# Two transformer layers on one core: other order of first loads, one bank for c and b_s, earlier splits after the values, a later gated norm, and the selection's choices inside the attentions

## The chip, the cores and the metric

The kernel runs on one core of one Trainium2 chip. The metric is the device time of one execution, in microseconds, from a run without or with the profiler; the profiler's span, from the first to the last instruction, is some 2 us shorter. PE is TensorE (PEld its weight loads), DVE VectorE, ACT ScalarE, POOL GpSimd, SP SyncE, whose queue issues every DMA.

## The reference

A first layer on x (1024 positions of 1024) projects x by `w_in` into a gated MLP part, a differential attention of 4 heads and a selective attention of 4 heads. The last two matter here:

```python
u = gelu(u); v = layer_norm(gelu(v).reshape(..., 4, 64), ln_g, ln_b)   # gated part: v is normed in groups of 64
out_a = u * (einsum('gts,bnsgc->bntgc', masked_w_s, v) + b_s)          # by blocks of 128 positions
score = einsum('bth,bths->bts', wi * idx_scale, relu(qi . ki))         # index scores, 8 heads of 32
score = where(allowed, score, -inf)
_, sel = lax.top_k(score, 256)                                         # ties: the first positions win
attention of 4 heads over the 256 selected keys of each query
```

Then come the output projection, layer norm, a gated FFN of 2816 and layer norm; a second layer, whose vectors depend on silu(c) @ w_cond, has a stick-breaking attention, a pooling mixer and another such FFN. All products are made of fp32 operands split in a high and a low part, three products each.

## The kernel before

Each engine's program is written out by hand as a list of calls (`pe_program`, `act_program`, `dve_program`, `pool_program`, `sp_program`, from L2734); semaphores join them. So the order on each engine is fixed, and an instruction that waits holds all behind it. All edits lie in the first fifth of the time.

**First loads** (`sp_first`, L647): x comes in eight blocks of 128 rows, x0 to x7. PE turns each (L564), ACT copies the high part (L575), DVE subtracts the low part (L582). Weights come as units of 128 x 1024: SP loads one into one of three `raw` buffers (L434), ACT copies its high part into one of five `wh` (L485), POOL subtracts for `wl` (L502). `sp_feed`, `act_feed` and `pool_feed` do this as far ahead as the buffers allow; a load waits for the split of the unit three before it, a split for the last use of the unit five before it. The third unit (the index keys) is loaded by four small DMAs. After x5, x6 and x7 the products of the three index units for positions 0 to 511 follow, then c and the gated part's w_s and b_s are turned (L676 to L685) and the other halves of the index products made. ACT applies Silu to c (L696), out of c's bank.

**Projections** (steps s = 0 to 47, `projects`): 0 to 7 give u and v of the gated part ("a"), 8 to 15 the values ("b"), 16 to 39 queries and keys, two halves to each unit, 40 to 47 the values of the selective attention ("c"). The list `turns` (L890) says in which order the five streams are called: 0 the selection, 1 the projections, 2 the gated norm (eight turns: four "var", four "norm", `NORM_STEPS`), 3 the four gated products, 4 first halves of the first ten projections. ACT copies each result out of its bank; for s from 16 to 39 DVE makes the low part `prl` (L997) and frees the bank. PE has four banks for projections. At the last step of a kind (m == 7) ACT begins with `act_feed(..., leave=1)`, which splits the units that follow.

**Selection** (stream 0): 20 score tiles, two at a step (PE L1038, ACT L1055 relu, DVE L1067 and L1070), then 31 steps of a binary search for the 256th score, a bit each: DVE counts four of the six blocks of queries (blocks 2 to 5; L1097), ACT two (6 and 7; L1089). Step 38 ends it. Then `dve_choose` (L1187) makes, for each block, five instructions over 128 (i + 1) columns: equal (L1192), running count (L1195), ties beyond need (L1198), below (L1202), bias (L1206). Blocks 2 to 5 follow at steps 40, 42, 44, 46, with `running` as the place of their counts, blocks 6 and 7 in the attentions, with `tcum`.

**Attentions** (`pe_attend`, `act_attend`, `dve_attend`, L1455 to L1507): 48 events, one to a place t; 0 to 7 are head 0 of the differential attention, 8 to 23 head 1 and pair 0 of the selective one in turn. At place t PE makes the logits of t (L1294), weighs the values for t - 4 (L1384) and turns the probabilities of t - 2 (L1358). DVE reads the logits of t out of their banks (L1319), ends the sums of t - 1 (L1336 to L1344), then, at places 1 to 10, makes one instruction of a choice. Block i's choice is read by event ("c", 0, i), from place 13 on.

Of the kernel before, what the change touches and what calls it, by code (L numbers as in the profile page):

```python
# [15 lines left out]
ACT = mybir.ActivationFunctionType  # L16
# [12 lines left out]
NRAW = 3  # L29
# [143 lines left out]
def build(nc, T, out):  # L173
    with ExitStack() as top:
# [93 lines left out]
        sg, powers = sb("sg", 128), sb("powers", 32)  # L268
        running = res[:, 7168:8192]

# [376 lines left out]
        def sp_first():  # L647
            sp.i.dma_start(con[:, :], T["consts"]).then_inc(*con_in.up("con", 16))
            for tb in range(8):
                if tb >= 6:  # L650
                    sp.wait_ge(*mm.after(("x", tb - 6, 1)))
                sp.i.dma_start(x_bufs[tb % 6], xd[128 * tb:128 * tb + 128, :]).then_inc(*x_in[tb % 6].up(("x", tb), 16))
                if tb == 3:
                    sp_feed(-1, NRAW)
            sp.i.dma_start(nd[:, :], T["dist"]).then_inc(*nd_in.up("nd", 16))
# [10 lines left out]
        def pe_first():  # L666
# [8 lines left out]
            pe.wait_ge(*small_in.after("c"))  # L675
            pe.i.transpose(bank[:, 0:8], score[0:8, 0:128], idn[0:8, 0:8]).then_inc(*mm.up("c"))  # L676
            bank = X["r"].open("ws")
            pe.wait_ge(*X["r"].prior("ws"))
            pe.wait_ge(*gmlp_in.after("bs"))
            for g in range(4):  # L680
                last = pe.i.transpose(bank[:, 128 * g:128 * g + 128], tmp[:, 128 * g:128 * g + 128], idn)
            last.then_inc(*mm.up("ws"))
            bank = X["r"].open("bs")
            pe.wait_ge(*X["r"].prior("bs"))
            pe.i.transpose(bank[:, 0:4], b4, idn[0:4, 0:4]).then_inc(*mm.up("bs"))  # L685

        def act_first():
            for tb in range(8):
                act_turn("x", tb, xh)
                if 3 <= tb < 6:  # L690
                    act_feed(-1, most=tb - 2)
                if tb >= 5:
                    act_index(0, tb - 5)
            act_feed(-1)
            act.wait_ge(*mm.after("c"))
            act.i.activation(cc[:, :], uses.held["c"][:, 0:8], ACT.Silu).then_inc(*av.frees(uses, "c"))  # L696

# [3 lines left out]
        def dve_first():  # L701
            for tb in range(8):
                dve_turn("x", tb, xh, xl)
                if tb >= 5:
                    dve_index(0, tb - 5)
            dve.wait_ge(*mm.after("ws"))
            dve.i.tensor_copy(wst, uses.held["ws"][:, :]).then_inc(*dv.frees(uses, "ws"))
            wv = wst[64:128, :].rearrange("p (g s) -> p g s", g=4)[:, :, 0:64]
            dve.wait_ge(*dv.now())
            dve.i.memset(wv, 0.0).then_inc(*dv.up("wst"))  # L710
            dve.wait_ge(*mm.after("bs"))
            dve.i.tensor_copy(bsc[:, 0:4], uses.held["bs"][:, 0:4]).then_inc(*dv.frees(uses, "bs"))

# [177 lines left out]
        for s in range(N_PROJECT):  # L891
# [4 lines left out]
            else:  # L896
                turns += [0, 1] if s < 39 or s % 2 == 0 else [1]
            if 2 <= s < 10:
                turns.append(2)
            if FIRST_BITS + 1 <= s < FIRST_BITS + 5:  # L900
                turns.append(3)
# [57 lines left out]
        def act_project():  # L959
            for s, (n, m, half) in enumerate(projects):  # L960
# [20 lines left out]
                if half is not None or m < 7 or s == N_PROJECT - 1:  # L981
                    act_feed(project_released(s))
                yield

# [17 lines left out]
        def sp_project():  # L1002
            for s, (n, m, half) in enumerate(projects):
# [11 lines left out]
                elif n != "a":  # L1015
# [3 lines left out]
                                   ).then_inc(*stage_out[s % 4].up(("v", s), 16))  # L1019
                if s == QK0 + 1:  # L1020
                    sp_gmlp()
# [130 lines left out]
        def dve_topk():  # L1152
# [29 lines left out]
            yield  # L1182
            for n in range(4):
                rest(dve_choose(n, running))
                yield
# [300 lines left out]
        def dve_attend():  # L1486

            last_choices = chain(dve_choose(4, tcum), dve_choose(5, tcum), repeat(None))
            for t in range(N_PLACES):
# [8 lines left out]
                if u is not None:  # L1498
                    dve_sums(u)
                    next(last_choices)  # L1500
                h = last_block(t, 5)
# [1407 lines left out]
```

## Time and profile before

| what | us |
|---|---|
| median of three runs (lowest, highest) | 2557.81 (2553.99, 2559.68) |
| the profiled execution, its own time | 2555.43 |
| its span | 2553.6 |
| PE busy in the span | 2416.5 (95%) |
| DVE busy | 1502.8 (59%) |
| ACT busy | 933.2 (37%) |
| POOL busy | 691.0 (27%) |
| mean granted clock of PE | 0.973 |

Busy times are those of the whole span; the stretches below each have a limit of their own. Granted clock 1.00 is 2.4 GHz, 0.50 is 1.2 GHz. An idle time in brackets with an arrow names what ended it.

### The profile page before, as it was taken

Reading aid. Unit: us, or ns where it says so; the run is one execution under the profiler, and the core shown is the slowest. Engines: PE = TensorE matmul, PEld = TensorE weight load, DVE = VectorE, ACT = ScalarE, POOL = GpSimd, SP = SyncE. Lnnn points to the kernel's source line nnn. Section 1 sums busy time; section 2 is a strip of 40 time slices with the busy share of each in tenths; the row PEclk is TensorE's granted clock in tenths of the full one; section 3 lists DMA queues with packets and bytes.
Section 4 is the critical chain, followed back from the end, with each engine's and each line's share of the span. In section 5 each row is a group of like instructions: output and inputs, shape, how many; then the busy total and the mean of one; then the engine's idle time right before and its main releaser. Section 6 shows DMA issues by size and latency. Waiting matters only on the chain.

```text
span 2553.6 us, 31471 instructions
## 1 busy us (share of the span) xinstructions
PE 2416.5 (95%) x12119; PEld 1954.8 (77%) x12119; DVE 1502.8 (59%) x2557; ACT 933.2 (37%) x1704; POOL 691.0 (27%) x389
## 2 busy tenths in 40 slices
PE   7989988889999999999999989888989999999998
PEld 6667877778888777778887866666768888888886
DVE  2698988762766777763239037775466555544225
ACT  3556636661223232332113225554433333232112
POOL 2012210001135444542223211011224454442220
PEclk9999988989999999999999999998989999999999
DMA  5014542213314454454222210001322223233233
GB/s 163 17 50 139 200 149 88 96 58 136 117 58 132 149 173 154 152 181 173 90 104 80 79 42 18 26 17 67 99 91 69 88 73 93 83 132 116 99 107 116
DMA packets 216717, 260.01 MB, mean 102 GB/s; under 512 B 16348, under 2 KB 145900, under 8 KB 216568
## 3 DMA queue, kind: packets, MB, share of 16 engines
q1 hardware_dynamic: 216568, 258.00, 30.8%
q8 instruction: 96, 1.57, 0.3%
q14 instruction: 53, 0.43, 0.1%
HBM read 198.14 MB, written 59.82 MB: 101 GB/s over the span
## 4 chain that ended last, share of the span: by engine, by line
PE 72%; DVE 17%; ACT 3%; DMA 3%; issue 2%; POOL 1%; SPq 1%; POOLq 0%; DVEq 0%; ACTq 0%
PE bank L545 9%; PE bank L547 9%; PE bank L546 9%; PE bank L1876 7%; PE bank L1877 7%; PE bank L1878 7%; PE bank L521 5%; PE bank L523 5%; PE bank L522 5%; DVE rest L2492 2%; PE bank L1384 2%; DVE junk L1097 2%; DVE res L1319 2%; PE bank L564 1%; DVE took L2497 1%
## 5 line engine op out<-in xcount | busy, mean ns | idle before, releaser
L502 POOL TENSOR_TENSOR wl<-raw,wh 128x1024 fp32r<-128x1024 f32 x117 | 298.1, 2564 | 1354.2 <-ACT wh L485 1354.1
L545 PE MATMUL bank<-wh,yh 128*128 128x512 f32 x768 | 301.5, 393 | 4.3 <-POOL wl L502 1.7
L547 PE MATMUL bank<-wh,yl 128*128 128x512 f32 x768 | 299.2, 390 | 0.0
L546 PE MATMUL bank<-wl,yh 128*128 128x512 f32 x768 | 299.2, 390 | 0.0
L497 POOL TENSOR_TENSOR wl<-res,wh 128x512 fp32r<-128x512 f32 x144 | 198.4, 1400 | 146.8 <-ACT wh L482 123.4
L485 ACT ACTIVATE wh<-raw 128x1024 fp32r<-128x1024 f32 x117 | 122.8, 1056 | 304.8 <-PE bank L547 287.1
L1876 PE MATMUL bank<-yh,wh 128*128 128x512 f32 x576 | 225.2, 391 | 0.0
L1878 PE MATMUL bank<-yh,wl 128*128 128x512 f32 x576 | 224.2, 389 | 0.0
L1877 PE MATMUL bank<-yl,wh 128*128 128x512 f32 x576 | 224.1, 389 | 0.0
L497 POOL TENSOR_TENSOR wl<-raw,wh 128x512 fp32r<-128x512 f32 x108 | 157.2, 1469 | 231.6 <-ACT wh L482 231.6
L2009 DVE TENSOR_TENSOR res<-bank,res 128x512 f32<-128x512 f32 x144 | 99.6, 692 | 136.2 <-PE bank L1878 128.4
L2075 DVE TENSOR_TENSOR res<-bank,res 128x512 f32<-128x512 f32 x96 | 65.0, 689 | 184.8 <-PE bank L547 184.8
L545 PEld LDWEIGHTS bank<-wh,yh 128*128 128x128 f32 x768 | 144.5, 188 | 36.6 <-issue 5.3
L547 PEld LDWEIGHTS bank<-wh,yl 128*128 128x128 f32 x768 | 144.3, 188 | 30.1
L546 PEld LDWEIGHTS bank<-wl,yh 128*128 128x128 f32 x768 | 144.5, 188 | 29.4
L521 PE MATMUL bank<-yh,wh 128*128 128x512 f32 x384 | 153.9, 401 | 2.9 <-DVE ql L2388 1.4
L482 ACT ACTIVATE wh<-res 128x512 fp32r<-128x512 f32 x144 | 83.5, 623 | 192.7 <-DVE res L469 141.6
L522 PE MATMUL bank<-yl,wh 128*128 128x512 f32 x384 | 151.0, 393 | 0.0
L523 PE MATMUL bank<-yh,wl 128*128 128x512 f32 x384 | 151.0, 393 | 0.0
L1876 PEld LDWEIGHTS bank<-yh,wh 128*128 128x128 f32 x576 | 108.1, 188 | 29.9 <-issue 4.3
L1878 PEld LDWEIGHTS bank<-yh,wl 128*128 128x128 f32 x576 | 108.1, 188 | 22.7
L1877 PEld LDWEIGHTS bank<-yl,wh 128*128 128x128 f32 x576 | 108.1, 188 | 22.1
(339 smaller groups left out, 5418.6 us busy)
## 6 DMA issues: line engine op xcount, KB each, us to landing
early<-in_w_cond SPq DMA_DIRECT2D x96, 256.0 KB, 2.9
raw<-in_w_gu SPq DMA_DIRECT2D x44, 512.0 KB, 4.1
raw<-in_w_down SPq DMA_DIRECT2D x44, 512.0 KB, 3.6
raw<-in_w_in SPq DMA_DIRECT2D x40, 512.0 KB, 4.2
qk_d<-res SPq DMA_DIRECT2D x36, 512.0 KB, 4.3
raw<-in_w_gate SPq DMA_DIRECT2D x22, 512.0 KB, 4.1
raw<-in_w_up SPq DMA_DIRECT2D x22, 512.0 KB, 4.3
res<-in_x SPq DMA_DIRECT2D x16, 512.0 KB, 8.6
```

What stands on the lines that cost most here:

```text
L485: act.i.activation(wh[n % NU][:, :], raw_of(u)[:, :], ACT.Copy).then_inc(*av.up(("wh", u)))
L497: pool.i.tensor_tensor(wl[n % NU][:, half], src, wh[n % NU][:, half].bitcast(F32), ALU.subtract).then_inc(*po.up(("wl", u)))
L502: pool.i.tensor_tensor(wl[n % NU][:, :], raw_of(u)[:, :], wh[n % NU][:, :].bitcast(F32), ALU.subtract).then_inc(*po.up(("wl", u)))
L521: pe.i.matmul(bank[:, :], a, a_h[:, s], start=k == 0, stop=False)
L522: pe.i.matmul(bank[:, :], a, a_l[:, s], start=False, stop=False)
L523: last = pe.i.matmul(bank[:, :], b, a_h[:, s], start=False, stop=k == 7)
L545: pe.i.matmul(bank[:, 0:wide], xa, h[:, c:c + wide], start=k == 0, stop=False)
L546: pe.i.matmul(bank[:, 0:wide], xa, l[:, c:c + wide], start=False, stop=False)
L547: last = pe.i.matmul(bank[:, 0:wide], xb_, h[:, c:c + wide], start=False, stop=k == nk - 1)
L1876: pe.i.matmul(bank[:, :], h[:, c:c + 128], high[:, k, :], start=k == 0, stop=False)
L1877: pe.i.matmul(bank[:, :], h[:, c:c + 128], low[:, k, :], start=False, stop=False)
L1878: last = pe.i.matmul(bank[:, :], l[:, c:c + 128], high[:, k, :], start=False, stop=k == 3)
```

## The change

First loads: one unit before x4, the second after x5, the third after x7 (before: three before x4). c's bank: b_s is turned into the same bank as c; DVE copies both out, and ACT's Silu works in place. Values' successors: at step 14 ACT also makes the splits that step 15 began with, after its two bits. The gated norm's turns move from steps 2 to 9 to steps 7 to 14, the gated products from 11 to 14 to 26 to 29, the stores of out_a from step 17 to step 30. Choices: all thirty instructions lie in `dve_attend`, with `tcum`, after the sums at places 5 to 22: min(30, 30 (t - 4) // 18) of them are made by place t.

```diff
@@ -266,7 +266,6 @@
         junk = sb("junk", 1024, BF, 512)
         junk_a = sb("junk_a", 1024, BF, 512)
         sg, powers = sb("sg", 128), sb("powers", 32)
-        running = res[:, 7168:8192]
 
 
         area(low)
@@ -650,8 +649,9 @@
                 if tb >= 6:
                     sp.wait_ge(*mm.after(("x", tb - 6, 1)))
                 sp.i.dma_start(x_bufs[tb % 6], xd[128 * tb:128 * tb + 128, :]).then_inc(*x_in[tb % 6].up(("x", tb), 16))
-                if tb == 3:
-                    sp_feed(-1, NRAW)
+                if tb in (3, 5):
+                    sp_feed(-1, tb // 2)
+            sp_feed(-1, NRAW)
             sp.i.dma_start(nd[:, :], T["dist"]).then_inc(*nd_in.up("nd", 16))
             sp.i.dma_start(score[0:8, 0:128], T["c_2"].rearrange("(k p) -> k p", p=128)).then_inc(*small_in.up("c", 16))
             for n, nm in ((0, "gmlp_ln_g"), (1, "gmlp_ln_b")):
@@ -673,16 +673,14 @@
             bank = X["r"].open("c")
             pe.wait_ge(*X["r"].prior("c"))
             pe.wait_ge(*small_in.after("c"))
-            pe.i.transpose(bank[:, 0:8], score[0:8, 0:128], idn[0:8, 0:8]).then_inc(*mm.up("c"))
+            pe.i.transpose(bank[:, 0:8], score[0:8, 0:128], idn[0:8, 0:8])
+            pe.wait_ge(*gmlp_in.after("bs"))
+            pe.i.transpose(bank[:, 8:12], b4, idn[0:4, 0:4]).then_inc(*mm.up("c"))
             bank = X["r"].open("ws")
             pe.wait_ge(*X["r"].prior("ws"))
-            pe.wait_ge(*gmlp_in.after("bs"))
             for g in range(4):
                 last = pe.i.transpose(bank[:, 128 * g:128 * g + 128], tmp[:, 128 * g:128 * g + 128], idn)
             last.then_inc(*mm.up("ws"))
-            bank = X["r"].open("bs")
-            pe.wait_ge(*X["r"].prior("bs"))
-            pe.i.transpose(bank[:, 0:4], b4, idn[0:4, 0:4]).then_inc(*mm.up("bs"))
 
         def act_first():
             for tb in range(8):
@@ -692,8 +690,8 @@
                 if tb >= 5:
                     act_index(0, tb - 5)
             act_feed(-1)
-            act.wait_ge(*mm.after("c"))
-            act.i.activation(cc[:, :], uses.held["c"][:, 0:8], ACT.Silu).then_inc(*av.frees(uses, "c"))
+            act.wait_ge(*dv.after("c"))
+            act.i.activation(cc[:, :], cc[:, :], ACT.Silu).then_inc(*av.up("c"))
 
         def pool_first():
             pool_feed(-1)
@@ -703,13 +701,14 @@
                 dve_turn("x", tb, xh, xl)
                 if tb >= 5:
                     dve_index(0, tb - 5)
+            dve.wait_ge(*mm.after("c"))
+            dve.i.tensor_copy(bsc[:, 0:4], uses.held["c"][:, 8:12]).then_inc(*dv.up())
+            dve.i.tensor_copy(cc[:, :], uses.held["c"][:, 0:8]).then_inc(*dv.frees(uses, "c"))
             dve.wait_ge(*mm.after("ws"))
             dve.i.tensor_copy(wst, uses.held["ws"][:, :]).then_inc(*dv.frees(uses, "ws"))
             wv = wst[64:128, :].rearrange("p (g s) -> p g s", g=4)[:, :, 0:64]
             dve.wait_ge(*dv.now())
             dve.i.memset(wv, 0.0).then_inc(*dv.up("wst"))
-            dve.wait_ge(*mm.after("bs"))
-            dve.i.tensor_copy(bsc[:, 0:4], uses.held["bs"][:, 0:4]).then_inc(*dv.frees(uses, "bs"))
 
 
 
@@ -895,9 +894,9 @@
                 turns += [0, 0, 1] if s % 2 else [0, 1]
             else:
                 turns += [0, 1] if s < 39 or s % 2 == 0 else [1]
-            if 2 <= s < 10:
+            if 7 <= s < 15:
                 turns.append(2)
-            if FIRST_BITS + 1 <= s < FIRST_BITS + 5:
+            if 26 <= s < 30:
                 turns.append(3)
         vbufs = [res[:, 6144 + 512 * i:6656 + 512 * i] for i in range(4)]
         staged = [b[:, :].bitcast(F32) for b in (*prh, *prl)]
@@ -980,6 +979,10 @@
                                      ).then_inc(*av.up(("project", s)))
                 if half is not None or m < 7 or s == N_PROJECT - 1:
                     act_feed(project_released(s))
+
+
+                if (n, m) == ("b", 6):
+                    act_feed(project_released(s + 1), leave=1)
                 yield
 
         def pool_project():
@@ -1017,7 +1020,7 @@
                     wide, c = (512, 0) if n == "b" else (256, 512)
                     sp.i.dma_start(T["v_d"][128 * m:128 * m + 128, c:c + wide], staged[s % 4][:, 0:wide]
                                    ).then_inc(*stage_out[s % 4].up(("v", s), 16))
-                if s == QK0 + 1:
+                if s == QK0 + 14:
                     sp_gmlp()
                 if s == QK0 + 5:
                     sp_load_head(0)
@@ -1180,8 +1183,7 @@
             dve.wait_ge(*dv.now())
             dve.i.tensor_scalar(need, cnt, -1.0, 256.0, ALU.mult, ALU.add).then_inc(*dv.up())
             yield
-            for n in range(4):
-                rest(dve_choose(n, running))
+            while True:
                 yield
 
         def dve_choose(n, sums):
@@ -1485,7 +1487,11 @@
 
         def dve_attend():
 
-            last_choices = chain(dve_choose(4, tcum), dve_choose(5, tcum), repeat(None))
+            choices = chain.from_iterable(dve_choose(n, tcum) for n in range(6))
+
+            def chosen_by(t):
+                return min(30, max(0, 30 * (t - 4) // 18))
+
             for t in range(N_PLACES):
                 if t < N_EVENT:
                     dve_logits(t, 0)
@@ -1497,7 +1503,8 @@
                 u = lagging(t, 1)
                 if u is not None:
                     dve_sums(u)
-                    next(last_choices)
+                    for _ in range(chosen_by(t) - chosen_by(t - 1)):
+                        next(choices)
                 h = last_block(t, 5)
                 if h is not None:
                     dve_subln(h)
```

## Rows read from the trace of the kernel before

**Rows 1.** The page: the span, and the chain that ended last by engine
```profile
span 2553.6 us, 31471 instructions
...
PE 72%; DVE 17%; ACT 3%; DMA 3%; issue 2%; POOL 1%; SPq 1%; POOLq 0%; DVEq 0%; ACTq 0%
```

**Rows 2.** Windows: busy us (and instructions) of each engine in six stretches
```profile
core 0: us, PE busy (x) PEld busy (x) DVE busy (x) ACT busy (x) POOL busy (x), PEclk, DMA share, GB/s
80.00:142.00 62.00, 61.41 (x432) 44.22 (x430) 50.31 (x91) 40.45 (x87) 0.00 (x0) 1.00 0.01 1
142.00:164.00 22.00, 15.61 (x102) 10.89 (x102) 20.20 (x24) 14.31 (x23) 10.26 (x4) 0.92 0.34 88
...
221.00:341.00 120.00, 120.00 (x526) 99.19 (x525) 102.69 (x282) 75.64 (x123) 32.63 (x14) 0.99 0.59 198
...
366.70:408.20 41.50, 30.56 (x180) 24.04 (x181) 37.75 (x96) 24.08 (x66) 4.17 (x2) 0.71 0.45 155
408.20:460.50 52.30, 46.65 (x350) 38.45 (x349) 39.70 (x131) 37.40 (x88) 0.00 (x0) 0.90 0.21 69
460.50:472.80 12.30, 12.05 (x102) 10.76 (x103) 4.17 (x22) 8.43 (x25) 0.00 (x0) 1.00 0.05 10
```

**Rows 3.** Timeline of the first loads: start, us, engine, line, [idle before <-releaser]
```profile
3.08 11.44 SPq L434 DMA_DIRECT2D raw<-in_w_in  x6
...
19.62 1.97 PE L564 MATMUL bank<-con,res 128*128 128x128 f32 x8 [4.47 <-DMA res<-in_x]
22.25 1.94 PE L564 MATMUL bank<-con,res 128*128 128x128 f32 x8 [0.65 <-DVE xl L582]
```

**Rows 4.** Timeline around c's Silu
```profile
45.49 1.28 ACT L696 ACT_TABLE_LOAD   x1
47.02 0.26 PE L685 MATMUL bank<-con,res 4*128 4x4 f32 x1 [3.33 <-ACT cc L696]
48.23 0.63 PE L523 MATMUL bank<-xh,wl 128*128 128x512 f32 x1
```

**Rows 5.** Timeline: the last of lambda's loads, and the reduction on DVE
```profile
52.38 0.43 SPq L1239 DMA_DIRECT2D sg<-in_diff_subln_g  x1
57.34 2.40 DVE L1245 CUSTOM_DVE_ANT_0 score<-score 128x64 f32<-128x64 f32 x1
```

**Rows 6.** Timeline: a norm step on DVE beside three splits on POOL
```profile
143.28 7.73 POOL L502 TENSOR_TENSOR wl<-raw,wh 128x1024 fp32r<-128x1024 f32 x3 [72.80 <-ACT wh L485]
147.03 0.69 DVE L815 TENSOR_REDUCE res<-res 128x8 f32<-128x512 f32 x1 [0.42 <-ACT res L968]
148.73 2.82 DVE L819 TENSOR_TENSOR res<-res 128x512 f32<-128x512 f32 x1
```

**Rows 7.** Timeline: a gated product, the successors' splits, and two waits
```profile
183.89 1.02 PE L861 MATMUL bank<-res 128*128 128x512 f32 x2
216.55 2.93 ACT L485 ACTIVATE wh<-raw 128x1024 fp32r<-128x1024 f32 x3
220.24 0.76 PE L521 MATMUL bank<-xh,wh 128*128 128x512 f32 x1 [6.26 <-POOL wl L502]
232.56 0.69 DVE L997 SCALAR_TENSOR_TENSOR prl<-bank,prh 128x512 fp32r<-128x512 f32 x1 [4.51 <-DMA v_d<-prl]
```

**Rows 8.** Timeline: first and last of 20 and of 10 choices; first logits
```profile
348.50 0.42 DVE L1192 TENSOR_SCALAR junk<-score,cand 128x384 bf16<-128x384 f32 x1
365.38 0.96 DVE L1206 SCALAR_TENSOR_TENSOR score<-score,nd 128x768 f32<-128x768 f32 x1
365.39 0.33 PE L1294 MATMUL bank<-kh,qh 64*128 64x128 f32 x2
366.26 0.28 DVE L1319 CUSTOM_DVE_ANT_0 res<-bank,nd 128x128 f32<-128x128 f32 x1
371.31 0.69 DVE L1192 TENSOR_SCALAR junk<-score,cand 128x896 bf16<-128x896 f32 x1
407.09 1.23 DVE L1206 SCALAR_TENSOR_TENSOR score<-score,nd 128x1024 f32<-128x1024 f32 x1
```

## The prediction

> **What bounds the kernel now.** I read the page first: a span of 2553.6 us whose last-ending chain is mostly TensorE (PE), with 17% of VectorE (DVE) [rows 1]. All edits lie before 475 us, so I cut that part into stretches and compared the busy time of the engines [rows 2]. From 80 to 142 us (score tiles and first projections) PE is busy 61.41 of 62 us: PE sets the pace, and what DVE does beside it is free. From 142 to 164 PE is busy 15.61 of 22 us and DVE 20.20: DVE sets it. From 221 to 341 PE is busy 120.00 of 120. In the attentions, 366.7 to 408.2 (places 1 to 10) has DVE at 37.75 of 41.5 us and PE at 30.56; 408.2 to 460.5 (places 11 to 23) has PE at 46.65 of 52.3 and DVE at 39.70. So each moved DVE instruction is worth what its old stretch gives back, less what its new one takes.
>
> **First loads: 3.8 us gained.** SP spends 3.08 to 14.52 us issuing three units of weights (six DMAs, four of them small pieces), and only then issues x4. PE idles 4.47 us and turns x4 at 19.62 [rows 3]. Now one unit is loaded ahead of x4 and x5. PE turned x3 at 13.2 and turns are 2.6 us apart (22.25 - 19.62, the row's start times), so x4 can be turned at 15.8: 3.8 us earlier. The third unit comes after x7, but its product starts only two products of 6.3 us after the first one, and its split takes 3.4 us.
>
> **c's bank: 5.7 us gained.** PE now waits 3.33 us before the turn of b_s (L685), since its bank holds c until ACT has loaded a table (1.28 us) and run Silu (L696) [rows 4]. After that the clock is at 1.2 GHz: twelve matmuls come every 0.427 us instead of 0.2275 (one of them is the 48.23 row), 2.4 us. With c and b_s in one bank, freed by a DVE copy, both go. What is late next is DVE: its lambda reduction waits for a load issued at 52.38 and then takes 2.40 us beside a split on POOL [rows 5], and it stands ahead of the copies that free PE's index banks. That load follows POOL's splits, which come 3.8 us earlier; the banks come free at about 56.1 and PE wants the first at 56.7. So the whole start gains 3.8 + 3.3 + 2.4 = 9.5 us, 6 if that chain is late.
>
> **The gated norm, later: a loss in DVE's chain.** Each of four variance steps holds four passes of 0.69 us and two small ones (3.2 us), each norm step three passes and a reciprocal (2.4 us); L815 is such a pass [rows 6]. Five steps, 14.4 us, run before 146.5 us under PE's cover. Moved behind step 7 of the projections they lose it: DVE would reach the end of that step's tiles near 143 (PE's own pace sets it, and the split on POOL that holds one pass) instead of 146.5, then owes 14.4 us more, in the stretch where DVE is the pace. The four gated products on DVE (3.0 us) leave this stretch. DVE's last bit of projection step 15 is then later by 14.4 - 3.5 - 3.0 = 7.9 us, at 226.2 instead of 218.3.
>
> **The successors' splits: the stall goes, another comes.** ACT splits three units at 216.55, after the two bits of step 15; PE stands idle 6.26 us until 220.24 [rows 7]. One step earlier this ends near 217.8 even with DVE's delay. But PE needs its banks back: the bank of projection 17 is freed by DVE after `prl` 17, which today waits 4.51 us for a store of v (DMA v_d<-prl, DVE at 232.56) [rows 7]. SP issues that store behind raw loads that wait for POOL's fourth split, and ACT makes this split after bit 16, about 12.6 us after the last bit of step 15. From 226.2 that is 238.8, and PE's projection 21 starts at 239.5 where it now starts at 237.8: a loss of 1.7 us in all, the saved stall included. Bounds: a gain of 7.5 (stall 6.3, cold matmuls 1.2) if DVE keeps up, a loss of 7 if it doesn't.
>
> **The gated products on PE: 3.5 us lost.** The four fp32 products (L861) make a projection last 6.34 us instead of 5.46, 0.88 each, now in a stretch where PE had slack (it stalled at 214 anyway) [rows 7]. At steps 26 to 29 PE has none [rows 2]: 4 x 0.88 = 3.5. The stores of out_a, now at step 30, are far ahead of their readers: nothing.
>
> **A collision: 2.3 us.** When three splits ran on POOL from 143.28 to 151.0, a DVE tensor_tensor (L819) took 2.82 us instead of 0.69 [rows 6]. The last norm step has three such passes and now starts near 215.6, where the three moved splits run; today these meet counts, which aren't held up. Each pass could lose about 1.8: 0 to 5.4 us, and I take 2.3, since the alignment is good to some us only. The Trainium skill (SBUF — State Buffer, Who interferes with whom) says that a DVE instruction with two SBUF inputs and a GpSimd instruction that reads SBUF lock each other out for a whole instruction. By that rule all three passes would wait, and the term would be 5.4; the L819 row agrees with it.
>
> The middle sums to 1.7 + 3.5 + 2.3 = 7.5 us lost, with bounds of 4 gained and 13 lost.
>
> **The choices.** Twenty instructions (blocks 2 to 5), 348.50 to 366.34, leave the end of the projections. There PE runs on until its first logits at 365.39, and DVE's first follows at 366.26 [rows 8]: they were covered, and at most 0.9 us comes back, counted at nothing. Ten more (blocks 6 and 7), 371.31 to 408.32, are in the attentions already [rows 8]; they last 13.0 us. Now all thirty, 17.1 + 13.0 = 30.0 us (by width a block costs 3.2, 3.9, 4.6, 5.4, 6.1, 6.8), are dealt over places 5 to 22, one, two, two, one and so on. Place by place, DVE's other work is what it was. Places 1 to 7 lose 9.1 us of choices and get 3.2: with PE's own limits (it runs at half clock there, mean 0.71 [rows 2]) 4.8 are gained. Places 8 to 10 are even. Places 11 to 23 get 23.0 and 0.7 of gaps, and of DVE's 12.6 us of idle there [rows 2] 9.4 are waits (the rest are gaps of 0.03 us between instructions): 14.3 lost. From place 24 to 27, DVE now waits for PE's backlog DVE busy 4.17 of 12.3 [rows 2]; PE will have less of it, which returns some 1.9. That leaves 14.3 - 4.8 - 1.9 = 7.6; PE's shadow of exp and turns at the wide places, and its clock, cost more. I add 2.4 for these, from one spell at 1.2 GHz as after b_s. The choices cost 10 us; bounds 4 (every idle used) and 18 (two or three more spells at half clock).
>
> **Sum.** -9.5 + 7.5 + 10.0 = +8.0 us. The profiled execution took 2555.43 us (1.8 around its span), so 2563.4; the median of the three runs is 2557.81, 2.4 above it, and on that base the forecast is 2565.8.
>
> **Rivals.**
> Chance 0.45: the forecast, DVE is the pace in both new places.
> Rival A, faster, 0.15: the idle time absorbs the choices. DVE has 3.75 us idle in 366.7 to 408.2 and 12.6 in 408.2 to 460.5 [rows 2], 16.4 together, nearly the 17.1 that come. If the attentions cost 2 and the middle 0, -9.5 + 2 = -7.5: 2550.3. Against it: the idle is in pieces between waits, the first part is not where choices land, and choices stand between sums and the next logits.
> Rival B, no change, 0.25: the attentions cost 10, but the middle is even, because the norm's 14.4 us fit into waits of DVE for PE or because the collision is missed: -9.5 + 0 + 10 = +0.5: 2558.3. It decides if `prl` 17 is not later against step 7 than now.
> Rival C, clearly slower, 0.15: PE, idle at places 12 and 13 where DVE gets 2.4 + 1.7 us of choices beside 3.9 + 5.5 of its own, falls to 1.2 GHz, then at places 19 to 23 too, where its work (4 to 6 us a place) doubles and PE becomes the pace. Three more spells at the 2.4 us of the one after b_s, and the full 5.4 of collision: 8.0 + 7.2 + 3.1 = +18.3, 2576.1. It decides when the granted clock of 408.2 to 460.5 falls below 0.85 (now 0.90).
>
> Faster by over 0.2% (5.1 us, about what a measurement here can tell from none): 0.15 (A). Within: 0.27 (B and a small part of the forecast). Slower: 0.58. The range holds the forecast, B and most of C: 2552.5 to 2576.
>
> **What would show it.** Right: x4's turn at 15.8, no gap before L685, the first scores 9.5 us earlier; the wait on `wl` at 220 gone but PE waiting for ACT's or DVE's bank frees around steps 17 to 21; L861 inside the full stretch; DVE at over 95% from place 8 to 23 and PE waiting for its logits and sums. Wrong: PE's first logits over 5 us earlier than 365.39 - 2.0, which would mean the norm cost nothing, or places 11 to 23 done in under 58 us (52.3 now, 66.6 by my sum). The forecast also fails if the start gains less: the score tiles' time tells that alone.

## The result and the profile after

The changed kernel took 2572.48 us (median of 4, 2571.34 to 2577.75) beside 2555.9 us for the kernel before: a ratio of 1.0068, 95% interval 1.0056 to 1.0080, some 17 us slower. Measured again with five runs, beside the experiments, it took 2571.43 us, 1.0057 (1.0044 to 1.0070). The forecast was 8.0 us slower. The time lies in the range, between the forecast (2565.8) and rival C (2576.1), and the distance from the forecast, 6.7 us, is nearly as large as the forecast loss. So this section asks for each term where its part of the other 7 to 9 us came from.

The page of the changed kernel, span and chain (for [rows 1]):
```profile
span 2576.0 us, 31465 instructions
...
PE 67%; DVE 21%; DMA 4%; ACT 3%; issue 2%; POOL 1%; SPq 0%; POOLq 0%; DVEq 0%; ACTq 0%
```
DVE's share of the chain that ended last rose from 17% to 21% and PE's fell from 72% to 67%: PE waits for DVE more often. This execution took 2577.75 us, the longest of its nine; the profiled one of the second measurement took 2573.23.

The windows of the changed kernel, to be read beside [rows 2]: the end of the score tiles, the search beside the first q and k products, and the attentions' places 1 to 10, 11 to 23, 24 to 26:
```profile
core 0: us, PE busy (x) PEld busy (x) DVE busy (x) ACT busy (x) POOL busy (x), PEclk, DMA share, GB/s
142.00:164.00 22.00, 17.34 (x90) 12.81 (x89) 20.05 (x30) 10.36 (x18) 3.37 (x2) 0.92 0.33 94
200.00:232.00 32.00, 19.77 (x67) 15.37 (x67) 29.98 (x72) 19.35 (x32) 9.36 (x4) 0.73 0.22 66
371.50:408.37 36.87, 28.48 (x178) 22.93 (x179) 31.78 (x97) 24.80 (x66) 3.80 (x2) 0.77 0.50 175
408.37:479.42 71.05, 54.66 (x351) 44.82 (x351) 62.29 (x151) 37.77 (x88) 0.00 (x0) 0.78 0.15 51
479.42:493.30 13.88, 13.65 (x102) 12.35 (x102) 4.11 (x21) 8.53 (x25) 0.00 (x0) 0.88 0.04 7
```
Places 11 to 23 last 71.05 us (52.3 before), with DVE at 62.29 (39.70) and the clock at 0.78 (0.90). From 200 to 232 PE works 19.77 of 32 us.

The three longest waits of PE between 140 and 230 us (engine, line waited for, us, times, longest):
```profile
PE bank L520 <- ACT prl L973: 7.6, 1, 7.6
PE bank L520 <- ACT prh L973: 6.9, 1, 6.9
PE bank L1041 <- ACT res L1058: 4.3, 1, 4.3
```
The wait for `wl` of [rows 7] has shrunk to 0.6 us. Two waits for a bank stand in its place, and both banks are freed by ACT's copies of v.

All kernels below are compared in three stretches, read from PE's rows of each trace: up to the first score matmul (78.53 us before), from there to the first logits (286.86), and from there to the logits of place 46 (176.82). The differences from the kernel before, in us; the last column is the ratio of the timed runs less one, times 2556, with its interval. The three stretches are those of one execution each: the first column differs by up to 1.7 us between kernels whose start is the same, and the sum of the three lies up to 5 us from the timed difference.

| kernel | start | middle | attentions | timed |
|---|---|---|---|---|
| changed kernel, first | -5.7 | +10.7 | +15.9 | +17 (14 to 20) |
| changed kernel, again | -6.3 | +10.7 | +14.0 | +15 (11 to 18) |
| choices alone | 0.0 | 0.0 | +12.1 | +13 (10 to 16) |
| choices alone, PE filled | -0.5 | +0.9 | +14.5 | +11 (8 to 14) |
| first loads and bank of c | -6.2 | +1.4 | -0.4 | -8 (-11 to -5) |
| splits | +1.0 | -7.2 | -0.7 | -9 (-12 to -6) |
| products | -0.5 | +1.6 | +0.4 | +2 (0 to 4) |
| norm and products | +0.5 | +13.2 | +0.3 | +9 (6 to 13) |
| norm, products and splits | +0.8 | +9.8 | -1.1 | +7 (4 to 10) |
| changed, choices as before | -6.0 | +10.4 | -1.0 | +1 (-1 to +4) |
| changed, norm as before | -7.2 | -5.4 | +12.3 | -4 (-7 to -1) |
| start and splits | -7.4 | -6.2 | +0.3 | -14 (-17 to -11) |
| the same, lambda later | -9.4 | -7.1 | +0.3 | -18 (-21 to -14) |

### The profile page after: what moved, and what is told of

Same layout as the page of the kernel before. It is cut to its first block, busy times and chain, and to the rows that moved or that the text cites. A ratio compares the mean times of both kernels' runs of the same rounds, so it can differ in the third digit from the quotient of the medians.

```text
span 2576.0 us, 31465 instructions
## 1 busy us (share of the span) xinstructions
PE 2423.8 (94%) x12119; PEld 1957.1 (76%) x12119; DVE 1505.5 (58%) x2558; ACT 923.3 (36%) x1698; POOL 690.1 (27%) x389
## 4 chain that ended last, share of the span: by engine, by line
PE 67%; DVE 21%; DMA 4%; ACT 3%; issue 2%; POOL 1%; SPq 0%; POOLq 0%; DVEq 0%; ACTq 0%
PE bank L544 9%; PE bank L546 9%; PE bank L545 9%; PE bank L1883 7%; PE bank L1884 7%; PE bank L1885 7%; DVE junk L1100 4%; PE bank L520 4%; PE bank L521 4%; PE bank L522 4%; DVE rest L2499 2%; PE bank L1386 2%; DVE res L1321 2%; PE bank L1296 1%; PE bank L563 1%
```

## The experiments

Each kernel below was run in five rounds beside the kernel before.

### The changed kernel again, and with the choices as before

The second kernel goes back on one part:
```
+        running = res[:, 7168:8192]
...
-            while True:
+            for n in range(4):
+                rest(dve_choose(n, running))
                 yield
...
-                    for _ in range(chosen_by(t) - chosen_by(t - 1)):
-                        next(choices)
+                    next(last_choices)
```

> The changed kernel itself, beside the runs of this set. The three parts alone gave +13.1 (choices), -8.5 (start) and +7.2 us (middle) at the medians, sum +11.8, where the changed kernel gave +17 over four runs. Theory 1: the parts add up and the first measurement was high by its own spread: +12 to +14. Theory 2: they don't add up, the attentions being dearer when the projections end later (the profile has a clock of 0.78 over places 11 to 23 there, 0.83 with the choices alone): +16 to +18.

> The changed kernel with the choices as before (five blocks' work after the last search step and one instruction at each of ten places). Theory 1 (parts add up): start and middle give -8.5 + 7.2, so -1.3 us against before. Theory 2: the start's gain is lost in the middle, where DVE's chain of counts sets the end of PE's waits, or the choices at the end of the projections no longer find cover, since DVE ends the search later against PE: +2 to +4.

Measured: 1.0057 (1.0044 to 1.0070) and 1.0004 (0.9995 to 1.0014). The first number puts the changed kernel 15 us (11 to 18) slower, between its two theories and compatible with both. The choices cost 13 us (2571.43 - 2558.14) in company of all other edits. In the second kernel start and middle together are 4.4 us slower in the trace and 1 in the timed runs. So Theory 1 of its expectation, that the parts add up to -1.3, isn't excluded by the times, but its trace has the start's gain more than spent by the first logits.

### The choices alone

```
-            for n in range(4):
-                rest(dve_choose(n, running))
+            while True:
                 yield
...
-                    next(last_choices)
+                    for _ in range(chosen_by(t) - chosen_by(t - 1)):
+                        next(choices)
```

> The kernel before with the choices alone changed (all thirty instructions dealt over places 5 to 22 of the attentions, none beside the last projections). Theory 1 (the forecast): DVE is the pace of places 11 to 23, so +10.0 us, with 66.6 us for places 11 to 23. Theory 2 (rival C, and what the changed kernel's trace hints at with 71.05 us for these places): PE is starved in pieces and its clock falls, so +15 to +18 and a granted clock under 0.85 over places 11 to 23. Rival A (idle time absorbs them): +2 or less. Were the choices dearer only in company with the other edits, this run would stay near +10 while the changed kernel's attentions cost 15.7.

Measured: 1.0051 (1.0039 to 1.0064), +13 us, between Theory 1 and Theory 2. The windows of this kernel, places 1 to 10 and 11 to 23, and what DVE waited for in the second:
```profile
366.70:402.95 36.25, 27.87 (x184) 22.61 (x185) 31.56 (x97) 24.25 (x66) 3.50 (x2) 0.81 0.50 178
402.95:471.46 68.51, 51.08 (x346) 41.88 (x344) 62.12 (x151) 37.97 (x89) 0.00 (x0) 0.83 0.16 53
```
```profile
DVE osc L1406 <- PE bank L1382: 2.7, 3, 1.0
DVE res L1317 <- PE bank L1292: 0.3, 1, 0.3
```
And DVE's waits in the kernel before, over the same places (408.6 to 460.7 us):
```profile
DVE res L1319 <- PE bank L1294: 5.1, 6, 1.8
DVE osc L1408 <- PE bank L1384: 4.9, 4, 1.9
```
DVE got 22.4 us more (62.12 less 39.70). Its waits for PE shrank from 10.0 to 3.0 us, so 7.0 us were absorbed, and 0.6 us of gaps came with twenty more instructions: 22.4 - 7.0 + 0.6 = 16.0, and the stretch is 16.2 longer than the 52.3 of [rows 2]. DVE is at work in 62.12 of 68.51 us and waits in 3.0; the rest are gaps of 0.03 us between its instructions. Rival A falls: the idle time took 7 of the 22.4 us. PE, for its part, waits for DVE. Its longest waits over the same places, with the choices alone and then in the kernel before (408.2 to 460.5):
```profile
PE bank L1292 <- DVE st L1317: 7.7, 4, 3.4
PE bank L1356 <- DVE res L1342: 4.4, 1, 4.4
```
```profile
PE bank L1358 <- DVE res L1344: 1.9, 1, 1.9
PE bank L1294 <- DVE st L1319: 0.8, 2, 0.6
```
The same sum holds in every kernel with the choices dealt over places 5 to 22: the length of places 11 to 23 less DVE's waits is 65.5 to 65.7 us in all five such traces, and 42.2 to 42.3 in all nine others. What changes from one execution to the next is how long DVE waits for PE: 3.0 us here, 4.7 and 5.5 in the two traces of the changed kernel.

### Is it PE's clock? The choices with PE filled

PE's matmuls in these places take 4.4 us longer than before (51.08 against 46.65 of busy time; the expectation below has 6.6), with the clock at 0.83 instead of 0.90, which is what rival C asks for. This kernel adds matmuls that nobody reads, into the next bank of the ring, ahead of PE's waits (the two tables say how many at which place, ahead of the turns and ahead of the logits; the calls are left out here):
```
+        def pe_warm(count):
+            if not count:
+                return
+            b = X["r"].bufs[X["r"].n % 4]
+            pe.wait_ge(*uses.freed.get(uses.latest.get(b.name), (None, 0)))
+            for _ in range(count):
+                pe.i.matmul(b[:, 0:512], stacks[1][0][0:64, 0:128], stacks[1][2][0:64, 0:512], start=True, stop=True)
...
+        WARM_OVER, WARM_LOGITS = {12: 14, 13: 5, 17: 3}, {15: 6, 19: 7, 21: 11}
```

> The kernel with the choices alone changed (+13.1 us), to which 46 matmuls of 512 columns are added that nobody reads, put where PE idles in places 12, 13, 15, 17, 19 and 21, just ahead of its waits. They change nothing but PE's activity, so that the granted clock of places 11 to 23 (0.83) comes back toward 0.90 or more. Theory 1: the slower clock is a part of the loss (PE's same matmuls took 6.6 us longer over these places): 3 to 5 us come back, the matmuls after the idle times being at full clock. Theory 2: DVE alone is the pace and PE's clock is of no account: within 1 us of the kernel without them at the start of place 24 on DVE.

Measured: 1.0043 (1.0030 to 1.0056), not told apart from 1.0051. Windows of the same places, first with PE filled, then (from 402.95) with the choices alone:
```profile
402.85:418.00 15.15, 14.34 (x84) 10.12 (x82) 14.59 (x40) 8.24 (x22) 0.00 (x0) 1.00 0.58 187
418.00:440.00 22.00, 18.70 (x95) 15.05 (x95) 17.86 (x50) 11.53 (x27) 0.00 (x0) 0.61 0.08 25
440.00:473.33 33.33, 27.50 (x211) 23.40 (x208) 29.70 (x64) 18.20 (x40) 0.00 (x0) 0.95 0.02 7
```
```profile
402.95:419.00 16.05, 11.29 (x67) 7.97 (x65) 15.19 (x41) 8.68 (x23) 0.00 (x0) 0.75 0.56 184
419.00:441.00 22.00, 18.71 (x119) 16.22 (x119) 20.12 (x50) 12.26 (x31) 0.00 (x0) 0.72 0.07 20
441.00:471.46 30.46, 21.08 (x161) 17.70 (x160) 26.80 (x62) 17.03 (x36) 0.00 (x0) 0.94 0.03 8
```
In the first stretch the clock went from 0.75 to 1.00, and no more than about 1 us came back, since DVE was busy in 14.59 of 15.15 us. But the clock fell all the same later, to 0.61 against 0.72, so over all of the places it rose only from 0.83 to 0.85. For places 12 and 13 this speaks against the clock as the price. For places 15 to 23 the edit didn't do what it was made for. All places together lasted longer than without it, 70.48 us against 68.51, because DVE waited for PE 5.0 us instead of 3.0:
```profile
DVE osc L1406 <- PE bank L1382: 3.4, 3, 1.4
DVE res L1317 <- PE bank L1292: 1.6, 1, 1.6
```
So the added matmuls, or the slower spell after them, stood in the way of real ones, and this kernel can't say what a faster clock alone would have given there. Neither theory of its expectation holds. What the clock costs can be bounded from above by DVE's waits for PE: they are 3.0 us with the choices alone, so no more than 3 us of the 13 can come from PE's clock over these places.

### First loads and bank of c; the lambda reduction

```
-                if tb == 3:
-                    sp_feed(-1, NRAW)
+                if tb in (3, 5):
+                    sp_feed(-1, tb // 2)
+            sp_feed(-1, NRAW)
...
+            pe.i.transpose(bank[:, 0:8], score[0:8, 0:128], idn[0:8, 0:8])
+            pe.wait_ge(*gmlp_in.after("bs"))
+            pe.i.transpose(bank[:, 8:12], b4, idn[0:4, 0:4]).then_inc(*mm.up("c"))
```

> The kernel before with the first loads' new order and the common bank of c and b_s, nothing else. Theory 1: the start gains 9.5 us and all of it reaches the end. Theory 2: the lambda chain on DVE holds the index banks and the start gains only about 6 (first scores at 72.8 instead of 78.5), all of it reaching the end: -6. Theory 3: the gain is eaten later, at the wait on the successors' splits near 214 to 220, since DVE's chain of counts sets their time: then -6 at the first scores and a smaller number at the first logits, unless DVE is as much earlier.

Measured: 0.9969 (0.9957 to 0.9981), -8 us; first scores 6.2 us earlier. Theory 2's mechanism holds, and Theory 3 perhaps in part: in this trace 1.4 us are lost before the first logits. In the changed kernel the same is seen, the turn of x4 and what stands where [rows 4] had the wait for c:
```profile
16.14 1.94 PE L563 MATMUL bank<-con,res 128*128 128x128 f32 x8 [0.65 <-DVE xl L581]
...
39.86 0.20 PE L678 MATMUL bank<-con,res 4*128 4x4 f32 x1
...
40.40 0.48 PE L520 MATMUL bank<-xh,wh 128*128 128x512 f32 x1
...
58.95 0.39 PE L737 MATMUL bank<-xh,wih 128*8 128x512 f32 x1 [1.93 <-DVE iql L771]
```
x4 is turned at 16.14 and there is no gap ahead of the turn of b_s. At 58.95 PE has waited 1.93 us for DVE's copy of an index bank, which stands behind the lambda reduction. The next kernel takes that away (it has the splits as well):
```
-            dve_lambda()
             dve_powers()
-            for n in range(3):
+            for n in range(2):
                 dve_index(1, n)
+            dve_lambda()
+            dve_index(1, 2)
             dve_lambda_end()
```

> The kernel before with the new first loads, the common bank of c and b_s and the earlier splits; norm, products and choices as before. If the start's gain (-8.5 measured alone) and the splits' gain are independent: -12 to -15 us. If DVE's chain of search steps is what both push against, it gives little more than the start alone: -8 to -9.

> The kernel before with the first loads, the common bank and the earlier splits (-14.1 us together), and DVE's order of the start changed besides: the list of powers and two index copies ahead of the lambda reduction. Theory 1: the reduction alone held PE's index bank (1.80 us idle, then ten matmuls at half clock), so 3 to 4 us more are gained: -17 to -18 us. Theory 2: the bank would be late in any case, ACT's copies standing behind its splits: no further gain, -14.

Measured: 0.9945 (0.9932 to 0.9958), 2543.02 us, for the first, so the two parts' gains nearly add; 0.9931 (0.9917 to 0.9945), 2539.67 us, with the reduction moved. PE's waits between 45 and 70 us, without and with that move:
```profile
PE bank L738 <- DVE iql L772: 1.8, 1, 1.8
```
```profile
PE bank L748 <- DVE score L787: 0.8, 1, 0.8
```
PE's wait for the index bank is gone, and the first score comes 9.4 us earlier than before, 2.0 earlier than without the move. That is the full 9.5 of the forecast, which needed one more edit than the change holds. The two timed intervals overlap; that the reduction held the bank is shown by the trace, a gain of 3 us in the time by the medians alone. This kernel, 16.7 us faster than the one before by the medians (2556.38), is the best of the study.

### Splits, products, norm

Four kernels: the first edit below alone, the second alone, the second and third together, and all three. (The norm can't be moved alone, since the products read what it leaves.)
```
+                if (n, m) == ("b", 6):
+                    act_feed(project_released(s + 1), leave=1)
```
```
-            if FIRST_BITS + 1 <= s < FIRST_BITS + 5:
+            if 26 <= s < 30:
                 turns.append(3)
...
-                if s == QK0 + 1:
+                if s == QK0 + 14:
                     sp_gmlp()
```
```
-            if 2 <= s < 10:
+            if 7 <= s < 15:
                 turns.append(2)
```

> The kernel before with only the three units after the v product split one step earlier. Theory 1: PE's wait of 6.26 us before the first q product shrinks to the time in which the third unit is split, and its cold matmuls go: -4 to -7.5 us. Theory 2: the product only starts earlier and waits a few products later for a bank, which DVE's search step frees (projection 21 at 237.8 as before): 0 to -1.

> The kernel before with only the four gated products (and their stores) moved from steps 11 to 14 to steps 26 to 29. Theory 1: PE pays 4 x 0.88 = 3.5 us where it has no slack, but DVE is 3.0 us lighter before the wait of PE at 214 to 220, which ends as much earlier: +0.5. Theory 2: the wait ends no earlier (PE's own earlier arrival only makes it longer): +3.5.

> The kernel before with the norm at steps 7 to 14 and the gated products at 26 to 29, but without the earlier splits. Earlier splits alone gave -9.2 us, all three edits together +7.2. Theory 1 (they add): norm and products cost 16 us on their own, so +14 to +17. Theory 2 (each loss has the same cause, PE's wait for a bank behind DVE's search): the earlier splits gain little once DVE is late, so norm and products cost only 8 to 10. Beside the time: if the stretched passes of the last norm step (2.8 us instead of 0.69) come from the splits on POOL, they aren't stretched here, where the splits run later.

> The kernel before with the norm's turns at steps 7 to 14, the gated products at 26 to 29 with their stores at step 30, and the three units after the v product split one step earlier; start and choices as before. Theory 1 (the forecast): +7.5 us. Theory 2 (what the changed kernel's first logits show, 370.4 against 365.4 with a start that gained 5.7): +10.7, since PE waits twice for a bank behind the counts (6.9 and 7.6 us) and not once. Rival B (the norm's 14.4 us fit into waits): 0.

Measured: splits 0.9964 (0.9952 to 0.9976), products 1.0008 (1.0000 to 1.0017), norm and products 1.0037 (1.0025 to 1.0049), all three 1.0028 (1.0017 to 1.0039).

Splits alone remove the wait of 6.26 us altogether: the trace has no wait of PE between 165 and 341 us, and from the first scores to the first logits it takes 7.2 us less. The product that the expectation's Theory 2 wanted to see waiting for a bank doesn't wait: DVE, not made late, keeps up.

Products alone: counted from the first scores, the wait ends 2.6 us earlier, since DVE has less to do, and from its end to the first logits it takes 4.2 us more, where PE has no slack (149.3 instead of 145.1 us; 3.5 of it was foreseen). The middle is 1.6 us longer.

Norm and products: PE waits 6.75 us at 203 and 12.51 us at 217, the second for the split, and the middle is 13.2 us longer. With the splits it is 9.8. So in the traces the splits are worth 7.2 us alone and 3.5 beside the late norm; in the timed runs the latter difference (9 against 7) is within the intervals. Of the two theories for the kernel with norm and products neither holds in full: +9 by the ratio speaks for the second, +12 by the medians and +13.2 in the trace for a value between.

The collision is plain in these kernels. The rows are two passes of the norm steps, L834 and L838, four times each, with least, median and greatest ns; first with norm and products alone, then with the splits too:
```profile
L834 DVE TENSOR_TENSOR res<-res x4: 692/692/693, 169.2 to 217.5; 128x512 f32<-128x512 f32 x4
L838 DVE TENSOR_TENSOR res<-res x4: 691/692/692, 170.0 to 218.2; 128x512 f32<-128x512 f32 x4
```
```profile
L834 DVE TENSOR_TENSOR res<-res x4: 691/692/2822, 169.5 to 217.8; 128x512 f32<-128x512 f32 x4
L838 DVE TENSOR_TENSOR res<-res x4: 691/694/2768, 170.3 to 220.7; 128x512 f32<-128x512 f32 x4
```
Without the three splits on POOL beside the last norm step no pass of it is held up; with them two are, 2.1 us each. Counted from the first scores, DVE's last bit of projection step 15 ends at 139.8 us before, at 148.9 in the one kernel and at 153.1 in the other: 9.1 and 13.3 us later, 4.2 apart, the two passes.

### The changed kernel with the norm as before

```
-            if 7 <= s < 15:
+            if 2 <= s < 10:
                 turns.append(2)
```

> The changed kernel with one thing undone: the norm's turns back at steps 2 to 9. Theory 1: the norm is the whole loss of the middle, since its 14.4 us of DVE work and the held-up passes lie in DVE's own chain; then this kernel is 14 to 16 us faster than the changed one, at +0 to +2 us against before (choices +13, start -8, splits -8, products +2). Theory 2 (the forecast's split of the loss): norm and collision cost 10 us and the rest is products and banks: +5 to +6 against before.

Measured: 0.9984 (0.9973 to 0.9995), so it is faster than the kernel before in spite of the choices. Against the changed kernel it gains 18.7 us by the two ratios (1.0057 and 0.9984) and 16.1 in the middle of the trace. The norm's place is the whole loss of the middle and more, as Theory 1 has it, whose sum of 0 to +2 us was still too high; the middle without it is 5.4 us shorter than before.

## Why the prediction was right or wrong

**Direction and rank of the causes: right.** The forecast had the start as a gain, the middle and the choices as losses, and DVE as the pace in both. All three are what the runs show. The gain of the start was taken too high by 2.1 to 3.8 us, the middle too low by 2.3 to 3.2, the choices by 2 to 6. The three errors have the same sign, so none hid another; the whole loss is about twice the forecast one.

**First loads and bank of c (forecast -9.5, measured -5.7 to -7.4 in the six traces with this start).** x4's turn was forecast for 15.8 and came at 16.14; the gap ahead of L685 and the matmuls at half clock after it went. The step that failed is "the banks come free at about 56.1 and PE wants the first at 56.7". PE wanted it at 57.02 and had it at 58.95. DVE's rows, first of the kernel before, then of the changed one:
```profile
57.34 2.40 DVE L1245 CUSTOM_DVE_ANT_0 score<-score 128x64 f32<-128x64 f32 x1
60.62 0.68 DVE L772 TENSOR_TENSOR iql<-bank,iqh 128x512 fp32r<-128x512 f32 x1
```
```profile
54.82 2.42 DVE L1247 CUSTOM_DVE_ANT_0 score<-score 128x64 f32<-128x64 f32 x1
58.12 1.28 DVE L771 TENSOR_TENSOR iql<-bank,iqh 128x512 fp32r<-128x512 f32 x2
```
56.1 is about where the reduction would end (59.74 less 3.8); the copy that frees the bank comes behind the list of powers, and its end before, 61.30, less 3.8 is 57.5, already too late. The chain also moved by 2.5 us only, not 3.8. The prediction named this case (6 if that chain is late), and took the other on a margin of 0.6 us. Behind the wait of 1.8 to 2.0 us, which all six traces have, four of them have eight matmuls in a row at half clock (0.43 us apart instead of 0.23, 1.6 us in all) and gain 5.7 to 6.3; the two without them gain 7.2 and 7.4. The kernel with the reduction moved shows 9.4, so the other terms of the sum were about right.

**The norm (forecast: DVE 7.9 us later at the last bit of step 15, plus 2.3 of collision).** Measured with all three edits: 13.3, of which 4.2 are the collision, so 9.1 against 7.9. The terms are near what was read. The eight steps are 24.8 us of work, one held-up step among them, where the kernel before has 10.5 left after step 7's tiles: 14.3 more. DVE is 3.1 us ahead at that point and not 3.5 (the norm starts 65.4 us after the first scores, where the kernel before stands at 68.5), and the products alone take 2.7 us off DVE's chain and not 3.0. That makes 8.5; the last 0.6 of the 9.1 I can't place.

**The path to PE: wrong line.** The prediction followed DVE's lateness to `prl` 17 and the bank of projection 21, and had the first q product start once the splits were done. In the trace PE starts that product well ahead (191.5 us), and then stands twice, at the second and the fourth of the q and k products, for banks that hold v. Timeline of the changed kernel, the second of these waits, from POOL's splits to PE:
```profile
209.16 7.56 POOL L501 TENSOR_TENSOR wl<-raw,wh 128x1024 fp32r<-128x1024 f32 x3 [56.37 <-ACT wh L484]
...
211.67 2.80 DVE L833 TENSOR_TENSOR res<-res 128x512 f32<-128x512 f32 x1
214.50 2.77 DVE L837 TENSOR_TENSOR res<-res 128x512 f32<-128x512 f32 x1
217.30 0.69 DVE L839 TENSOR_TENSOR res<-res 128x512 f32<-128x512 f32 x1
...
222.12 1.04 ACT L1092 ACTIVATE junk_a<-score,cand 128x896 bf16<-128x896 f32 x1 [8.15 <-DVE cand L1178]
...
224.44 0.58 ACT L973 ACTIVATE prl<-bank 128x512 f32<-128x512 f32 x1
...
225.07 0.80 PE L520 MATMUL bank<-xh,wh 128*128 128x512 f32 x1 [7.64 <-ACT prl L973]
```
Read upward: PE waits for a bank; ACT copies v out of it, but ACT stood 8.15 us before its counts, which wait for DVE's threshold; and DVE was in the norm, with two passes held up by the splits. ACT's copy needs nothing from DVE. It is late because it stands behind the counts in ACT's order. The "would show" list had PE waiting for ACT's or DVE's bank frees around steps 17 to 21, which fits (steps 17 and 19). But the term of 1.7 us was worked out at another place, and the first of the two waits had no term at all. That the middle still came within 3.2 us is in part luck: the lateness of DVE was right, the line on which PE pays for it was not. The upper bound of 13 for the middle holds the collision at 2.3; with the prediction's own 5.4 it would be 15.9.

**The splits (forecast bounds: a gain of 7.5 to a loss of 7).** The upper bound was right: 7.2 alone. The condition that the prediction gave for it, if DVE keeps up, is what the four kernels show.

**The collision (forecast 2.3 of 0 to 5.4).** Measured 4.2: two of the three passes, at 2.80 and 2.77 us. The Trainium skill (SBUF — State Buffer, Who interferes with whom) has a DVE instruction with two SBUF inputs and a GpSimd instruction that reads SBUF lock each other out for a whole instruction. The trace agrees with it: both passes that began while the splits ran lasted about one split (7.56 us for three), and the third began after them, at 0.69. The forecast of 2.3 hedged on the alignment; the norm step came at 217.6 in the kernel with the middle's edits alone, 2 us later than the 215.6 of the prediction, and the splits ran from 215.34 to 222.92.

**The products (forecast 3.5, set against 3.0 less on DVE).** Alone they cost 1.6 us of trace, 0 to 4 timed: 4.2 set against 2.6. The terms were right within 0.7.

**The choices (forecast +10.0).** By its steps, in the kernel with the choices alone, on DVE's rows: places 1 to 10, forecast -4.8, measured -5.4 (36.6 us instead of 42.0 from DVE's first logits); places 11 to 23, forecast +14.3 and 2.4 for clock and waits, measured +16.2, because 7.0 us of waits were absorbed and not 9.4; places 24 to 26, forecast -1.9, measured +1.7. Together 12.5, so most of the miss of 2.5 lies in the last term. The backlog whose shrinking was to give 1.9 back gave nothing: PE is busy 13.66 of 13.90 us there, at a clock of 0.88 (before 12.01 of 12.26, at 1.00). All five traces with dealt choices have 13.9 us here; of the nine others seven have 12.3 and two 13.9, so this much comes from the clock of the execution at least in part.

In the changed kernel the choices took 14.0 and 15.9 us in two executions. Places 11 to 23 were 1.7 and 2.5 us longer there than in the kernel with the choices alone, and DVE's waits for PE were longer by as much, with PE's busy time for the same matmuls at 53.99 and 54.66 us against 51.08:
```profile
DVE osc L1410 <- PE bank L1386: 4.6, 3, 2.5
DVE res L1321 <- PE bank L1296: 1.0, 2, 0.7
```
These are the waits of the slower execution, to be compared with the 2.7 and 0.3 above. That the lower clock (0.78 and 0.81 against 0.83) made them longer is likely, but these are three executions only.

**The rivals.** A fell with the 7.0 us absorbed. B decides by `prl` 17, which was later (164.4 us after the first scores in the kernel with the middle's edits, 154.0 before); it fell. C's own test was met, with a granted clock of 0.78 to 0.83 where it asked for less than 0.85, and its time is nearer to the measured than the forecast's. Its explanation, that PE becomes the pace, is not what the traces show: DVE's own work, with the short gaps in it, makes up 65.5 us of these places in every execution, and PE's lateness adds 3.0 to 5.5. The measured sum is the forecast's mechanism with larger terms: -6 for the start, +10.7 for the middle, +14 to +16 for the attentions, 18.4 to 20.9 at place 46, where the timed runs say 15 to 17.

**The signs.** Of those named for being right, two failed: the first scores came 5.7 us earlier and not 9.5, and DVE was busy 88% of places 11 to 23 (62.29 of 71.05 us) and not over 95%. Of those named for being wrong, the smaller gain of the start came. The other two did not: the first logits are 5.0 us later than before (370.42), and places 11 to 23 took 71.05 us, where under 58 would have spoken against the forecast and 66.6 was its own sum.

## What to carry to other kernels

A step moved off a stretch where PE is the pace onto one where a search on DVE is costs its full length, and whatever ACT does after that search's counts is late with it; follow the lateness through the other engines' orders to each bank that PE wants, not to one only. When such a stretch varies between executions, take the pace-setting engine's waits off its length: here what was left agreed within 0.2 us in five traces. Follow a chain to the very instruction that frees the bank, and where two chains end within a microsecond of each other in a sum, take the worse one and ask what could be moved out of it: here a lambda reduction, whose move brought the first scores 2.0 us forward. Combine only the parts that pay when run alone: start, splits and the reduction together gave 17 us where the whole change lost 17.

## What was not expected of the hardware

The same stretch of the same kernel, places 11 to 23 of the changed kernel, lasted 71.05 us at a granted clock of 0.78 and 70.18 at 0.81 in two executions; with the norm as before it lasted 69.07 at 0.83. Filling PE's idle time with 46 matmuls, 19 of them at places 12 and 13, brought the clock of that first stretch from 0.75 to 1.00, and in the next it fell to 0.61, lower than without them (0.72). The same wait of PE near 57 us, 1.8 to 2.0 us long, was followed by eight matmuls at half clock in four traces (granted clock from 60 to 69 us 0.81 to 0.86) and by none in two (1.00).
